# A hybrid decoder step: prompt attention moved into the recurrent heads, the last sample's scores under the last projection tiles, a value ring of seven pages

## The reference

```python
def even_mix(h, pos, w_in, w_out, gn, lb, s0, attn):
    z = h @ w_in
    qa, fa, ia, ga, qb, kb, vb = jnp.split(z, ...)
    logf = jnp.logaddexp(jnp.log(lbh), jnp.log1p(-lbh) + jax.nn.log_sigmoid(heads(fa, H_A)))
    ka = -jnp.expm1(logf)
    va = jax.nn.silu(heads(ia, H_A))
    oa, S = gla_scan(heads(qa, H_A), ka, va, logf, s0)
    oa = head_rms_norm(oa, gn) * jax.nn.sigmoid(ga)
    qb, kb = rope(qb, ...), rope(kb, ...)
    ob = attn(qb, kb, vb)
    return jnp.concatenate([oa, ob], axis=-1) @ w_out, S, kb, vb

def gla_scan(...):                     # per chunk of 64 tokens
    b = jnp.cumsum(lc, axis=2)
    att = einsum('bhtd,bhsd,bhtsd->bhts', qc, kc, exp(b_t - b_s))     # s <= t
    o = einsum('bhcd,bhde->bhce', qc * jnp.exp(b), S) + att @ vc
    S = exp(b_last) * S + (kc * jnp.exp(b_last - b))^T @ vc
```

## Time and profile before

| what | value |
|---|---|
| median of three runs | 3144.7 us (3142.7 to 3145.04) |
| the profiled execution | 3140.24 us, span 3138.6 us |
| granted clock of PE, mean of the span | 0.946 |
| busy over the span | PE 2846.4 us (91%), DVE 2160.5 (69%), ACT 1498.3 (48%), POOL 144.2 (5%) |
| E_IN, last evacuation | 455.1 us |
| attention pairs | 467 to 523.7 us |
| selection | 524.25 to 552.2 us |
| first gates, first `QE` | 568.1 us |
| eight heads | 568.1 to 850.9 us |
| first product of E_OUT | 853.28 us |

### The profile page before, as it was taken

How to read it: one execution, slowest core, us unless ns; L and a number is a source line. 1 busy time by engine, 2 the same in 40 slices (tenths; PEclk the granted TensorE clock), 3 DMA queues, 4 the chain that set the end, 5 groups by cost and what they waited for, 6 DMA issues and landing times.

```text
span 3138.6 us, 70433 instructions
## 1 busy us (share of the span) xinstructions
PE 2846.4 (91%) x22723; PEld 2683.6 (86%) x22723; DVE 2160.5 (69%) x5865; ACT 1498.3 (48%) x2828; POOL 144.2 (5%) x277
## 2 busy tenths in 40 slices
PE   7888883676799999999999999999699999999997
PEld 7788872344499999999999988888599999999997
DVE  4799978777766677757756665666566677657656
ACT  4333322333356755545545445454357755545444
POOL 0111101222100000000000000000000000000000
PEclk9899986687899999999999999999799999999999
DMA  6598955677755565556655565656365555566654
GB/s 220 204 319 313 313 192 170 220 256 260 244 184 167 181 186 180 182 180 180 186 170 187 186 228 190 218 197 215 138 181 167 186 181 181 181 181 181 186 170 138
DMA packets 181550, 627.56 MB, mean 200 GB/s; under 512 B 19536, under 2 KB 40416, under 8 KB 177104
## 3 DMA queue, kind: packets, MB, share of 16 engines
q1 hardware_dynamic: 135056, 449.74, 45.3%
q0 software_dynamic: 37920, 138.97, 13.1%
q10 hardware_dynamic: 8480, 37.59, 3.3%
HBM read 597.50 MB, written 28.73 MB: 200 GB/s over the span
## 4 chain that ended last, share of the span: by engine, by line
PE 73%; DVE 18%; issue 5%; ACT 3%; DMA 1%; DVEq 1%; ACTq 0%; SPq 0%; POOL 0%; POOLq 0%
PE stream L471 22%; PE stream L472 22%; PE stream L473 22%; DVE kring L1267 5%; DVE wlo L1144 4%; PE stream L538 1%; PE mix L680 1%; DVE Sb L1267 1%; PE mix L598 1%; DVE ze L1185 1%; PE mix L687 0%; PE stream L546 0%; DVE Aatt L1380 0%; DVE va L1335 0%; ACT whi L818 0%
## 5 line engine op out<-in xcount | busy, mean ns | idle before, releaser
L1144 DVE TENSOR_TENSOR wlo<-raw,whi 128x512 fp32r<-128x512 f32 (+1 forms) x1696 | 1098.6, 678 | 549.5 <-ACT whi L818 537.9
L818 ACT ACTIVATE whi<-raw 128x512 fp32r<-128x512 f32 (+1 forms) x1696 | 1013.2, 619 | 955.9 <-PE stream L473 827.0
L471 PE MATMUL stream<-hA_hi,whi 128*128 128x264 f32 x2688 | 787.6, 293 | 76.8 <-DVE ze L1185 39.9
L471 PE MATMUL stream<-hB_hi,whi 128*128 128x264 f32 x2816 | 800.9, 284 | 3.8 <-DVE ab L1205 3.8
L472 PE MATMUL stream<-hB_lo,whi 128*128 128x264 f32 x2816 | 799.2, 284 | 0.0
L473 PE MATMUL stream<-hB_hi,wlo 128*128 128x264 f32 x2816 | 798.8, 284 | 0.0
L472 PE MATMUL stream<-hA_lo,whi 128*128 128x264 f32 x2688 | 774.6, 288 | 0.0
L473 PE MATMUL stream<-hA_hi,wlo 128*128 128x264 f32 x2688 | 773.5, 288 | 0.0
L471 PEld LDWEIGHTS stream<-hA_hi,whi 128*128 128x128 f32 x2688 | 519.3, 193 | 104.4 <-DVE wlo L1144 59.5
L471 PEld LDWEIGHTS stream<-hB_hi,whi 128*128 128x128 f32 x2816 | 531.8, 189 | 4.3 <-DVE wlo L1144 4.2
L472 PEld LDWEIGHTS stream<-hB_lo,whi 128*128 128x128 f32 x2816 | 532.1, 189 | 0.1
(11 more groups left out here) (323 smaller groups left out, 2706.4 us busy)
## 6 DMA issues: line engine op xcount, KB each, us to landing
raw<-in_w_f_in SPq DMA_DIRECT2D x352, 512.0 KB, 3.7
kring<-in_cache_k POOLq DMA_DIRECT2D x128, 512.0 KB, 5.3
raw<-in_w_f_o SPq DMA_DIRECT2D x128, 512.0 KB, 3.6
raw<-in_w_odd_in SPq DMA_DIRECT2D x128, 512.0 KB, 4.2
raw<-in_w_even_in SPq DMA_DIRECT2D x112, 512.0 KB, 6.2
raw<-in_cache_v POOLq DMA_DIRECT2D x64, 512.0 KB, 5.4
vring<-in_cache_v POOLq DMA_DIRECT2D x64, 512.0 KB, 5.2
raw<-in_w_f_o SPq DMA_DIRECT2D x64, 384.0 KB, 3.5
```

Of the source, the lines that this page charges most:

```text
L471: mm(bank, hi, p.src[0][:, kt, :], start=first, stop=False)
L818: A(whi[:, 4 * j + k, 0:n], raw[:, 4 * j + k, 0:n], ACT.Copy).then_inc(hi_done, 1)
L1144: v.tensor_tensor(wlo[:, 4 * j + k, 0:n], raw[:, 4 * j + k, 0:n], whi[:, 4 * j + k, 0:n].bitcast(F32), ALU.subtract).then_inc(lo_done, 1)
```

## The change

- Prompt attention: the pairs and their copies of q and v are gone. Each `hgrn_head` h now works attention head h: scores after the level products, softmax after the level sums, scaling after the sample states, outputs before the head's own; all in one bank, `st[1]`.
- Sample 7 is scored under the last four E_IN tiles, four pages to a tile.
- One ACT pass over all heads makes silu and sigmoid in place, behind the last tile; the table for exponential and logarithm is then loaded once. Per-head reciprocals and their neighbours go.
- `KE` and the `kd` product go: the key's factor is folded into the exponent (`cdec`, one add). The seven-level reduction becomes three adds.
- The gates of head 0 stand inside `select_blocks`; those of head h+1 are spread over head h, and its `QE` stands before the output's last steps.
- The value ring has seven slots, none of them in `raw`. `EL`, `Sst`, `S0` and the small rows lie over `raw` instead, so E_OUT's first loads wait for four places of the last head.
- POOL issues the three constants right behind the stores of K and V, ahead of the value pages, and DVE waits for them before `select_blocks`.
- The heads are unrolled; prompt and sample states have store semaphores of their own.

```diff
-VSLOTS = 8
+VSLOTS = 7
...
+            def raw_released(half):
+                if half == 0:
+                    sp.wait_ge(HP.sem, HP.at("lev1", HEADS - 1))
+                elif half == 1:
+                    sp.wait_ge(HP.sem, HP.at("o", HEADS - 1))
+                    sp.wait_ge(hp_stored, 16 * HEADS)
+                elif half == 2:
+                    sp.wait_ge(HP.sem, HP.at("kv_b", HEADS - 1))
+                    sp.wait_ge(o8_ready, DEC)
+                else:
+                    sp.wait_ge(hs_stored, 16 * HEADS)
...
             def value_pages(b, first, last):
 
                 if first == 0:
                     pe.wait_ge(pb_ready, b + 1)
+                    if b:
+                        pe.wait_ge(om_ready, 4 * b)
...
-                pe.wait_ge(HV.sem, HV.at("pr1b", h))
+                pe.wait_ge(HV.sem, HV.at("att1", h))
...
+            act.wait_ge(tile_free, ZE)
+            A(ze[:, Z_IA:Z_IA + HEADS, :], ze[:, Z_IA:Z_IA + HEADS, :], ACT.Silu).then_inc(gates_squashed, 1)
+            A(ze[:, Z_GA:Z_GA + HEADS, :], ze[:, Z_GA:Z_GA + HEADS, :], ACT.Sigmoid).then_inc(gates_squashed, 1)
+            nc.scalar.preload_act_table_set("natural_log_exp_and_others")
...
+                    v.tensor_tensor(cdec[:, :], bcum[par][:, :], g2[:, 0:SEQ], ALU.add).then_inc(GV.sem, GV.one("c"))
...
-                    dve.wait_ge(HV.sem, HV.at(f"pr{c}b", h))
-                    v.tensor_reduce(Aatt[:, c, :], pr[:, :, :].rearrange("p l t -> p t l"), AX_X, ALU.add)\
-                        .then_inc(HV.sem, HV.one(f"att{c}"))
+                    v.tensor_tensor(pr[:, 0:3, :], pr[:, 0:3, :], pr[:, 4:7, :], ALU.add).then_inc(HV.sem, HV.one(f"fold_a{c}"))
+                    dve.wait_ge(HV.sem, HV.at(f"fold_a{c}", h))
+                    v.tensor_tensor(pr[:, 0:2, :], pr[:, 0:2, :], pr[:, 2:4, :], ALU.add).then_inc(HV.sem, HV.one(f"fold_b{c}"))
+                    dve.wait_ge(HV.sem, HV.at(f"fold_b{c}", h))
+                    v.tensor_tensor(Aatt[:, c, :], pr[:, 0, :], pr[:, 1, :], ALU.add).then_inc(HV.sem, HV.one(f"att{c}"))
+                attention_softmax(h)
+                if more:
+                    hgrn_gates(h + 1, 0)
+                    hgrn_gates(h + 1, 1)
...
+                attention_scale(h)
+                if more:
+                    hgrn_gates(h + 1, 2)
...
-            for i in (26, 27):
-                for j in range(2):
-                    lo_tile(E_IN, i, j)
-                    evac(E_IN, i - 1, j)
+            dve.wait_ge(q_copied, DEC)
+            for n in range(4):
+                lo_tile(E_IN, 26 + n // 2, n % 2)
+                evac(E_IN, 25 + n // 2, n % 2)
+                for g in range(4 * n, 4 * n + 4):
+                    score_page(DEC - 1, g)
...
-            dve.wait_ge(q_copied, DEC)
-            with dve.Fori(0, HEADS // 2) as i:
-                attention_pair(i)
...
+            dve.wait_ge(unit_used, 4 * ZE)
+            dve.wait_ge(hc_landed, 48)
+            dve.wait_ge(gates_squashed, 2)
             select_blocks()
             dve.wait_ge(SV.sem, SV.before(1))
-            dve.wait_ge(hc_landed, 48)
-            for piece in range(3):
-                hgrn_gates(0, 0, piece)
```

More of the change, by code:

```diff
@@ L157, in hybrid_step @@
         vec = sb("vec", [P, V_ALL])
+        with ExitStack() as part:
+            v_spare0 = sb("v_spare0", [P, HEADS * P], F32, part)
         rstd = sb("rstd", [P, TOK])
@@ new lines, in attention_scores, with attention_values @@
+            def attention_scores(h):
+                pe.wait_ge(BV.sem, BV.before(h))
+                pe.wait_ge(BA.sem, BA.before(h))
+                q_, k_ = ze[:, Z_QB + h, :], ze[:, Z_KB + h, :]
+                mm(st[1][:, 0:P], q_[:, 0:P], k_[:, 0:P], start=True, stop=False, skip_group_check=True)
+                mm(st[1][:, P:384], q_[:, P:SEQ], k_[:, 0:SEQ], start=False, stop=True, skip_group_check=True)\
+                    .then_inc(BP.sem, BP.one("scores"))
+            def attention_values(h):
+                pe.wait_ge(BV.sem, BV.at("masked", h))
+                for c in range(2):
+                    ins = tr(st[1][:, c * P:(c + 1) * P], ze[:, Z_VB + h, c * P:(c + 1) * P], ident[:, :])
+                ins.then_inc(BP.sem, BP.one("v_turned"))
@@ L750, in _ @@
             pe.wait_ge(SV.sem, SV.before(1))
-            with pe.Fori(0, HEADS // 2 - 1) as i:
-                for j in range(2):
-                    hgrn_head(i * 2 + j, j)
-            for j in range(2):
-                hgrn_head(HEADS - 2 + j, j)
+            for h in range(HEADS):
+                hgrn_head(h)
+            pe.wait_ge(BV.sem, BV.before(HEADS))
+            pe.wait_ge(BA.sem, BA.before(HEADS))
             pe.wait_ge(HV.sem, HV.before(HEADS))
@@ L1083, in _ @@
             act.wait_ge(kv_stored, 32)
+            act.wait_ge(om_ready, 4 * DEC)
             for j in range(2):
@@ L1318, in hgrn_gates, with attention_softmax @@
-            def hgrn_gates(h, par, piece):
-                f = tile(ze, h + Z_FA)
+            def attention_softmax(h):
+                dve.wait_ge(BP.sem, BP.at("scores", h))
+                v.tensor_tensor(sm[:, :], st[1][:, 0:384], cau[:, :], ALU.add).then_inc(BV.sem, BV.one("masked"))
+                dve.wait_ge(BV.sem, BV.at("masked", h))
+                for k, (a, b) in enumerate(((0, P), (P, 384))):
+                    v.tensor_reduce(mx2[:, k:k + 1], sm[:, a:b], AX_X, ALU.max).then_inc(BV.sem, BV.one(f"max{k}"))
+                dve.wait_ge(BV.sem, BV.at("max1", h))
+                v.tensor_scalar(nmx[:, :], mx2[:, :], -(P ** -0.5), None, ALU.mult).then_inc(BV.sem, BV.one("negmax"))
```

424 lines of the change are left out of this document (179 added, 245 removed).

## The result

The changed kernel takes 3044.7 us (median of four runs, 3042.2 to 3048.4), against 3144.7 before: a ratio of 0.9684, 95% interval 0.9673 to 0.9696. The forecast was 3045. The profiled span is 3041.5 us, 97.1 shorter than before.

| stretch | before, us | after, us | difference | forecast |
|---|---|---|---|---|
| to the start of the last four projection tiles | 428.2 | 430.7 | +2.5 | 0 |
| to the projection's last evacuation | 26.9 | 39.7 | +12.8 | +13 |
| key rotation | 11.7 | 11.7 | 0 | 0 |
| attention pairs | 56.9 | 0 | -56.9 | -56.9 |
| `qk` to the clearing of `cmp` | 0.5 | 11.0 | +10.5 | +9.6 |

A forecast was written before the change was run, and what follows sets the result against it. The prediction took the stream of weights and key pages to bound the kernel before 400 us and a relay of DVE and PE the heads. Its terms summed to -98.9 us, giving 3045 us on the median, range 3014 to 3076.

The forecast's parts named there:

- Projection tiles: Last four projection tiles with sample 7's pages: DVE decides at 9.56 us a tile, +13 us; up to +16 if not.
- The new wait: Before clearing `cmp`, DVE waits for three constants queued behind the K and V stores: +9.6 us, ends 4.1 and 12.
- Selection and first gates: Block selection takes in the first head's gates, +1.2 us; the separate stretch up to `QE` vanishes, -15.9 us.
- From the heads on: Everything after the heads, from E_OUT to the end: nothing differs, 0 us.
- Heads, DVE: DVE's work per head period: 22.5 us busy, a period of 25.4 where PE is never late.
- Heads, PE and the clock: PE's work per head: 22.3 us at full clock, 27.9 at 0.80; period 28.5 between ends of 25.4 and 31.9.
- half a slow stretch: PE before `om`: a whole stretch at the low clock costs about 5.3 us more a period; half was taken.
- the ends of the heads: Time before the first and after the last of the seven head periods: 33.4 us, from 34.4.
- Heads, the late pages: In each head period: 0.5 us allowed for value pages that come late.
- The ring of seven: Rival, chance 0.02: the value slots' round trip binds the heads; period 43 would give 3150 us.
- transfers did not decide: Rival, chance 0.18: low clock or transfers decide the heads' period, 32 to 35 us, giving 3070 to 3090 us.

The follow-up runs named there:

- run without scoring: Changed kernel with the scoring of the last sample's sixteen pages left out, the pages still loading: 3032.4 us, one run.
- half pages: Changed kernel with all value pages after the first seven loaded in their first half only: 3040.8 us, one run.
- filler and half pages: Changed kernel with eight unused identity products in PE's wait before the chunk states, and value pages after the first seven half loaded: 3030.6 us, one run.
- run with filler: Changed kernel with eight unused identity products on PE in its wait before the chunk states: 3040.9 us, ratio 0.9676.

## Why the prediction was right, and where it was right by luck

*Projection tiles* (+13): 12.8, and DVE never waited inside a tile. The forecast had let DVE decide and thought the transfers covered, which is right. The run without scoring shows that loading the pages is the next limit, only 6.5 us below.

*The new wait* (+9.6): 10.64, and issuing the three constants ahead of the stores takes it away. Their place behind the stores was the cause, in two parts that no run separates: POOL issued the last constant 2.4 us after DVE had come to wait, and it took 7.9 us to land instead of 3.8. The size was in part luck. The forecast took it from the second store, which had landed in 10.0 and now landed in 7.6.

*Selection and first gates* (+1.2, -15.9): 1.0 and 15.9.

*From the heads on* (0): -3.0. "From there on nothing differs" was wrong by the table load at the end of E_OUT, 1.28 us, and what went with it.

*Heads, DVE*: 22.5 busy us were worked out and 22.7 measured, the three adds and the softmax among them. The rule of the Trainium skill's page "VectorE: DVE Perf Modes", section "The perf-mode tier table", weighed there, would have made the adds lose; putting the reduction back cost 13 us, and 1.69 us for each reduction against 1.28 busy for three adds. The run and the page differ, and the run decides for this strided reduction.

*Heads, PE and the clock*: half a slow stretch was a middle between two ends, and the period came out at 28.8 for 28.5; the ends of the heads were 33.1 for 33.4. The clock was between its ends, 0.85. Half of the mechanism is as forecast: PE has to wait for DVE, and the low clock follows. The place is not. The forecast left PE idle before its output products, where the kernel before had waited for the running states:

```profile
658.74 1.22 PE L590 MATMUL mix<-Aatt,hv 128*128 128x128 f32 x4 [3.23 <-DVE Sst L1389]
```

In the changed kernel PE does not wait there; it waits 2.1 us a head before the chunk states, for DVE's level sums, and is then busy up to the pick. That the middle fell so close was chance: PE's stretch varies from head to head between 13.2 and 14.7, and over the runs from 11.5 to 16.4.

*Heads, the late pages*: 0.5 was allowed. PE waited for pages in few places; half pages gained 0.3 a period. The ring of seven did not bind, and the transfers did not decide; but both stand close behind, as filler and half pages together show. The 358 GB/s of the Trainium skill's page "DMA: Bandwidth & Descriptors", section "Specifications", were again passed for short stretches (397 over 4 us, 423 over 3 us in the run with filler); over seven whole periods no run here shown went above 335, so as a sustained limit it was not put to the test.

*What was not in the working*: the wait for the level sums before the chunk states, the chain from the pick to `qdec` over PE and ACT, and that PE's work in a gap can be worth more than its absence. None of them changed the sum, since the period was taken between ends and not from the chain. Not tried: to put PE's columns and first two pages, 4.0 us of that chain, behind the turns.

## What to carry to other kernels

Where two engines hand work back and forth, follow the chain through one turn before moving anything: the wait with the most microseconds belonged to it, but DVE's output steps, which stood right behind that wait, were at most one of two paths of nearly the same length. A wait that can be tied to the last reader of a buffer, and not to the end of the computation, is worth checking on each engine; one such name gave 17 us here. Small loads that a later stage waits for go ahead of large stores on the same queue; here that brought the first comparison 7.1 us forward, though the kernel's own 4 us are not told from none.

## What the runs showed of the hardware that I had not expected

In these heads PE's clock made a wait cost more than its length, and work cheaper than none: the same 1619 products took 170.2 us at a mean clock of 0.91 and 182.3 at 0.85; chunk states released 1.35 us earlier made a period 1.7 shorter; and with 1529 products, the attention left out, the seven periods took 209.1 us against 202.5 with it, in one run. Filling a 2 us wait with useless products kept 1.00 behind it at the place shown, where 0.50 had been granted for 6 us. Why the low clock follows some waits and not others I have not shown.

A reduction of 128x896 across seven levels took 1.66 to 1.78 us, the three adds in its place 0.56, 0.43 and 0.29.

Three constants issued behind two stores of 1056 KB landed in 7.3 to 7.9 us; issued ahead of them, in 2.3 to 3.8.
